# GpSimd subtracts each weight chunk's low half in four operations of 256 columns instead of one of 1024

## What is computed

```
x += 0.5 * SwiGLU_a(rms(x))
P = rms(x) @ w_in                      # one projection for all branches
A = retention(P[ret]);  B = SSD / Mamba-2(P[ssm]);  C = RWKV-7(P[rwkv])
x += w_out( sum_i sigmoid(P[gate_i]) * (branch_i @ w_branch_i) )
x += CrossAttn(rms(x), memory K/V)
x += 0.5 * SwiGLU_b(rms(x))
```

## Time and profile before

| what | value |
|---|---|
| profiled execution, its own time | 3634.34 us |
| span of that execution | 3632.8 us |
| mean granted TensorE clock | 0.922 |
| TensorE matmul busy | 3066.9 us (84%) |
| VectorE busy | 1950.2 us (54%) |
| ScalarE busy | 1166.7 us (32%) |
| GpSimd busy | 536.3 us (15%), of it 430.1 us in L675 |

### The profile page before, as it was taken

How to read it: one execution, slowest core, us unless ns; L and a number is a source line. 1 busy time by engine, 2 the same in 40 slices (tenths; PEclk the granted TensorE clock), 3 DMA queues, 4 the chain that set the end, 5 groups by cost and what they waited for, 6 DMA issues and landing times. The chain is left out here.

```text
span 3632.8 us, 63834 instructions
## 1 busy us (share of the span) xinstructions
PE 3066.9 (84%) x25648; PEld 2795.0 (77%) x25648; DVE 1950.2 (54%) x2906; ACT 1166.7 (32%) x1579; POOL 536.3 (15%) x337
## 2 busy tenths in 40 slices
PE   8999788877787889699989997888777869887997
PEld 7989577676576888499989895776765759885997
DVE  4437565584556455344344376665845655553543
ACT  4432421042121444244244324211421313432542
POOL 0005330143220000000000063201422200000000
PEclk9999899997798999899989998999988979999998
DMA  4434310124162445334344443101332724453442
GB/s 163 148 131 143 95 57 3 48 93 147 61 253 107 145 173 186 128 128 149 117 142 146 135 140 100 40 3 58 107 130 61 271 82 168 170 189 128 133 150 102
DMA packets 119680, 448.00 MB, mean 123 GB/s; under 512 B 13648, under 2 KB 23920, under 8 KB 112176
## 3 DMA queue, kind: packets, MB, share of 16 engines
q1 hardware_dynamic: 98496, 331.84, 27.9%
q0 software_dynamic: 20976, 113.24, 8.0%
HBM read 397.01 MB, written 48.02 MB: 123 GB/s over the span
## 5 line engine op out<-in xcount | busy, mean ns | idle before, releaser
L1359 ACT ACTIVATE w_high<-ring 128x1024 fp32r<-128x1024 f32 x598 | 632.0, 1057 | 953.2 <-PE gemm_banks L823 619.6
L821 PE MATMUL gemm_banks<-in_high,w_high 128*128 128x320 f32 (+1 forms) x2784 | 871.9, 313 | 78.0 <-POOL w_low L675 30.3
L822 PE MATMUL gemm_banks<-in_low,w_high 128*128 128x320 f32 (+1 forms) x2784 | 860.6, 309 | 0.0
L823 PE MATMUL gemm_banks<-in_high,w_low 128*128 128x320 f32 (+1 forms) x2784 | 860.2, 309 | 0.0
L1700 DVE TENSOR_TENSOR w_low<-ring,w_high 128x1024 fp32r<-128x1024 f32 x436 | 534.0, 1225 | 543.1 <-ACT w_high L1359 539.2
L821 PEld LDWEIGHTS gemm_banks<-in_high,w_high 128*128 128x128 f32 x2784 | 529.8, 190 | 95.0 <-issue 72.6
L675 POOL TENSOR_TENSOR w_low<-ring,w_high 128x1024 fp32r<-128x1024 f32 x162 | 430.1, 2657 | 1102.3 <-ACT w_high L1359 587.7
L822 PEld LDWEIGHTS gemm_banks<-in_low,w_high 128*128 128x128 f32 x2784 | 530.3, 190 | 1.1
L823 PEld LDWEIGHTS gemm_banks<-in_high,w_low 128*128 128x128 f32 x2784 | 529.5, 190 | 0.0
L861 PE MATMUL gemm_banks<-in_high,w_high 128*128 128x320 f32 x640 | 227.3, 355 | 76.1 <-ACT stage L1427 37.4
L813 PE MATMUL gemm_banks<-in_high,w_high 128*128 128x320 f32 (+1 forms) x656 | 210.7, 334 | 69.2 <-ACT in_high L1375 66.0
(11 more groups left out here) (383 smaller groups left out, 4530.8 us busy)
## 6 DMA issues: line engine op xcount, KB each, us to landing
ring<-in_w SPq DMA_DIRECT2D x602, 512.0 KB, 3.3
arena<-in_kc POOLq DMA_DIRECT2D x16, 1024.0 KB, 7.0
arena<-in_vc POOLq DMA_DIRECT2D x16, 1024.0 KB, 9.1
out_fill<-stage SPq DMA_DIRECT2D x80, 160.0 KB, 3.8
arena<-out_fill POOLq DMA_DIRECT2D x4, 2560.0 KB, 11.1
arena<-in_ssm POOLq DMA_DIRECT2D x16, 512.0 KB, 10.4
out_s_ssm<-arena POOLq DMA_DIRECT2D x16, 512.0 KB, 7.0
arena<-in_ret POOLq DMA_DIRECT2D x16, 512.0 KB, 23.2
```

The costliest lines, as they stand in the source:

```text
L821: mm(dst, w_high[:, slot, w(k)], in_high[:, k, 0:n], start=(k == 0), stop=False)
L822: mm(dst, w_high[:, slot, w(k)], in_low[:, k, 0:n], start=False, stop=False)
L823: ins_ = mm(dst, w_low[:, slot, w(k)], in_high[:, k, 0:n], start=False, stop=(k == KT - 1))
L1359: f(w_high[:, slot], ring[:, s, 0:D], ACT.Copy).then_inc(weights_high, 1)
```

## The change

The one subtraction of 1024 columns becomes four of 256, written one behind the other. Only the first has the wait for ScalarE's copy in front of it, and only the last raises `weights_split`, so TensorE is released at the same point of the work as before: when the whole chunk is subtracted. What VectorE subtracts is left as it is.

```diff
+PIECES = 4
@@ weights (GpSimd)
                 slot = RANK[pos] % AHEAD
                 pool.wait_ge(weights_high, i * unit + (RANK[pos] + 1))
-                nc.gpsimd.tensor_tensor(w_low[:, slot], ring[:, pos % RING, 0:D], w_high[:, slot].bitcast(F32),
-                                        ALU.subtract).then_inc(weights_split, 1)
+                for q in range(PIECES):
+                    c = slice(q * D // PIECES, (q + 1) * D // PIECES)
+                    ins_ = nc.gpsimd.tensor_tensor(w_low[:, slot, c], ring[:, pos % RING, c], w_high[:, slot, c].bitcast(F32),
+                                                   ALU.subtract)
+                ins_.then_inc(weights_split, 1)
```

## The result

The kernel with four pieces took 3646.86 us (median of 10 runs, 3639.19 to 3662.03) against 3639.51 for the kernel before on the same chip (10 runs). The ratio is 1.0026, 95% interval 1.0014 to 1.0039: 9.5 us slower, 5 to 14. The forecast was 33 us slower; the side was right, the size was not.

The account below looks back on a forecast made before the run. It took chunk matmuls, ScalarE's copy and GpSimd's subtraction as the bounding loop, with GpSimd and VectorE taking turns. Terms 10.8 + 7.0 + 9.0 + 7.0 = 33.8 us on 3634.3 gave 3668 us, range 3640 to 3702.

Parts of the forecast that it names:

- f = 0.15 us: Fixed cost of each added GpSimd operation; three more per chunk cost 0.45 us.
- The rival that the next piece starts up for nothing: GpSimd starts each piece while the last runs, no fixed cost, only turns: 3643 us, chance 0.15.
- Projection +10.8: In the `rwkv` projection, 24 chunk starts waiting for the subtraction each come 0.45 us later: 10.8 us.
- `prepare_rwkv`, +7.0: RWKV preparation: start -1.9, middle +1.0, end +4.4, making 3.5 us per layer, 7.0 for both.
- L1833 ends 1.8 us earlier and the sum L933 starts 1.9 us earlier: Preparation's start: VectorE waits 4.4 us instead of 6.1, so TensorE's waiting sum gains 1.9 us per layer.
- The middle, +1.0: Preparation's middle: four turns with L1844 make a fill 1.6 us late, of which the next column sum passes on 1.0.
- The end, +4.4: Preparation's end: pieces wait for L1862 and L1863, the fill starts 5.1 us late; 4.4 per layer after VectorE's lead.
- Headnorm's end and `ssm`, +9.0: Headnorm's end and the `ssm` projection: a start 2.1 us late plus later waits, 4.5 us per layer, 9.0 for both.
- 7 x 0.45 = 3.2: In the `ssm` projection, seven starts of L821 waiting for the subtraction each come 0.45 us later, per layer.
- Scan, +7.0: SSD scan: six L2033 groups 1.8, `z` load 0.9, two end fills 0.8; 3.5 us per layer, 7.0 for both.
- each of the four waits for one piece: the same 2.2 us in all: SSD scan: four L2033 operations wait as long together as one did for a whole subtraction, plus 0.3 us fixed per group.
- the one with VectorE's gain: Shorter VectorE waits at L933 and headnorm's end gain 5.4 us per layer: kernel faster at 3623 us, chance 0.10.

Follow-up runs that it names:

- proj: Four pieces only in the 26 chunks of the rwkv projection, whole elsewhere, against the kernel before: 1.0030, +11 us (6 to 16).
- e_end: Four pieces only in chunks 13 and 14 of the rwkv fills, beside VectorE's two great reductions, against the kernel before: 1.0029, +11 us (6 to 15).
- ssm: As a run: four pieces only in the 13 chunks of the ssm projection, against the kernel before: 1.0023, +8 us (4 to 12).
- sfill: Four pieces only in the 20 fill chunks in the SSD scan and first 2 of ret, against the kernel before: 0.9996, -1.5 us (-7 to +4).
- rfill: Four pieces only in the 20 fill chunks beside RWKV preparation and headnorm, against the kernel before: 1.0011, +4 us (-1 to 9).
- e_front: Four pieces only in chunks 2 to 4 of the rwkv fills, against the kernel before: 0.9979, -8 us (-13 to -3).
- e_mid: Four pieces only in chunks 5 to 12 of the rwkv fills, against the kernel before: 1.0003, +1 us (-3 to +5).
- before again: The kernel before, executed once more with a profile and no edit: 3636.78 us.
- e_fs: Four pieces only in chunks 2 to 4 of the rwkv fills and beside the SSD scan, against the kernel before: 0.9967, -12 us (-17 to -8).

## Why the forecast was wrong in size, by its own steps

**f = 0.15 us: right.** The shortest operations are 192, 712, 1252 and 2333 ns for 8, 256, 512 and 1024 columns: 2.11 ns a column and 0.17 us fixed. Of the latter some 0.04 overlap with the operation before when it is queued behind one. Four end to end take 2.82 us for 2.41 (forecast 2.75 to 2.85), so three pieces more cost 0.41 us, forecast 0.45. The estimate by the Trainium skill (GPSIMD Engine Reference, Performance versus the Vector engine), 169 ns from its 4497 ns for 2048 columns, agrees with the 0.17. The rival that the next piece starts up for nothing is out but for the 0.04.

**Projection +10.8: right.** +10.0 in the trace to L924, +11 in `proj`. The count behind it was off: 11 starts of a chunk a layer waited for GpSimd before and not 12 (of the 28 of L821 in the earlier trace rows, 12 are here and 16 in `ssm`), and 22 x 0.45 is 9.9. The period went from 7.47 to 7.87 (forecast 8.0), which the pieces' 0.41 us make up alone; nothing of it is left for L1806. What was forecast of it, a maximum under 1 us, was wrong; source view:

```profile
L1806 DVE SCALAR_TENSOR_TENSOR arena<-arena,par x52: 235/554/5761, 280.7 to 2187.9; - x48, 128x8 f32<-128x8 f32 x4
```

its median fell from 1277 to 554 ns, but the longest is 5761.

**`prepare_rwkv`, +7.0: +1.6 in the trace** (-5.4 + 6.2 and -5.5 + 6.3). The step that failed is "L1833 ends 1.8 us earlier and the sum L933 starts 1.9 us earlier". L1833 (now L1837) ended 3.3 us earlier against L1829's start, and the sum, its gap of 3.55 us gone, ran at a granted clock of 1.00, the upper level of 2.4 GHz. The windows are of before over 420.20 to 427.50 and of after over 419.70 to 424.27, each from the sum's start to the same matmul of the fill behind it; the columns are us, busy time of PE, PEld, DVE, ACT and POOL, granted clock, DMA share, GB/s:

```profile
420.20:427.50 7.30, 7.30 (x12) 3.25 (x13) 0.00 (x0) 0.00 (x0) 2.15 (x1) 0.64 0.03 7
```

```profile
419.70:424.27 4.57, 4.57 (x14) 2.18 (x13) 0.00 (x0) 1.38 (x2) 4.57 (x7) 1.00 0.54 154
```

that is 2.7 us more, which the forecast left out. The middle, +1.0, came out at -0.6: from the start of L1839 to that of L1860 (now L1864) it took 35.2 us for 35.8. The eight L1848 take 7.50 us for 10.85 (eight turns at 0.35 for three at 2.1), but a fill there waits 3.09 us for the chunk itself, at 450.50, where the earlier trace rows have 2.11. The end, +4.4, was a real loss, and larger. The walk itself was right to 0.1 us: against the start of L1860 (now L1864) the fill came at 10.69 us for 5.09, 5.6 later. But that fill, behind 7.23 us of idle time, ran at the lower clock, so the next one was 6.8 later and not 5.1. RWKV's start came 6.8 later too; with the middle's -0.6 these are the stage's 6.2. In `e_end`, with pieces in the end's two chunks alone, layer 1 has 6.9.

**Headnorm's end and `ssm`, +9.0: +4.3 in the trace, +8 (4 to 12) in `ssm` alone.** The start at 758.55 was further off than the 2.1 forecast. The last fill ahead of the projection already starts 3.5 us later than before (753.36 for 749.87) and that start 8.1 later (766.66), so 4.6 belong to this place, 2.5 of them to the first chunk's lower clock, 6.19 us for 3.68. Then the step "7 x 0.45 = 3.2" failed: the waits behind that start did not grow, their sum fell from 11.5 to 9.8 us. The convolution's first 45 operations on VectorE take 34.2 us for 38.4; that TensorE's waits fell by way of ScalarE's copies, which follow them, fits this but no run shows it apart. The 0.8 that I took back for this was too little. `ssm` timed alone, though, leaves the 9.0 inside its interval.

**Scan, +7.0: -10.7 in the trace, -1.5 (-7 to +4) timed alone.** This is the step with the largest error, and it has the wrong sign in the trace: "each of the four waits for one piece: the same 2.2 us in all". A group of four meets three turns, and a turn costs VectorE 0.35 us, not 0.55. So about half of a piece's 0.71 us goes by beside VectorE's operation. That is more than its fixed 0.17, and which part of it that is, no run shows. Before, one turn was 1.6 us where L2033 takes 352 ns alone (four of them took 1.96 us), now three are 1.0. For TensorE that is 2.1 us over both layers: its matmuls of L1104 waited 47.0 us for L2033 before and wait 44.9 for L2037 now. From the source views of the two, before and after:

```profile
  PE gemm_banks L1104: 26.3, 6
...
  PE mixer_banks L1104: 20.7, 10
```

```profile
  PE gemm_banks L1108: 23.0, 6
  PE mixer_banks L1108: 21.9, 11
```

So the scores, forecast at +3.6 for both layers, came to -2.1. These 2.1 are the edit's: `sfill` has the same 44.9, and `proj`, `ssm`, `rfill`, `e_front` and `e_mid`, with whole chunks there, have 46.9 to 47.2. Most of the 10.7 is something else, and the forecast had no term for it: TensorE is busy 8.0 us less over the same work (windows over the scan of both layers, before and after):

```profile
sum 362.30, PE 283.26 PEld 232.32 DVE 190.12 ACT 75.97 POOL 86.66; mean PE 141.63 PEld 116.16 DVE 95.06 ACT 37.98 POOL 43.33
```

```profile
sum 351.62, PE 275.28 PEld 226.55 DVE 183.61 ACT 75.97 POOL 111.92; mean PE 137.64 PEld 113.28 DVE 91.81 ACT 37.98 POOL 55.96
```

It goes with a granted clock of 0.82 and 0.83 in place of 0.79 and 0.80. An unedited kernel can have a part of this by chance: in layer 1 "before again" is busy for 140.0 us for 143.2, at 0.80. The five kernels with four pieces there are alike, -6.9 to -7.6 in layer 1 and -3.3 to -4.5 in layer 2; the seven with whole chunks have -3.2 to 0.0 and -0.3 to +3.1, so with the clock the edit's share is some 4 to 6 us a layer in the traces. Timed, it is -1.5 us (-7 to +4) by itself and -4 from `e_front` to `e_fs`, which is nearer to the 2.1 of the waits alone. Whether the shorter waits bring the better clock with them, and why the times show so little of it, stays open.

**Of the rivals**, the one with VectorE's gain had a place and the mechanism of what came: L933, worth 5.4 us a layer rather than 1.9. It was wrong on the point from which it decides: the fills behind L1862 were late, and it was outweighed. GpSimd didn't keep VectorE out through all four pieces: L1866 and L1867 got in between.

The sum by the trace: 10.0 + 1.6 + 4.3 - 10.7 = 5.2, -1.9 in the lora and +5.2 in the other stages, of which the forecast had neither: 8.5 in all. At the two places where shorter holds count most, the front and the scan, the forecast had -3.8 + 7.0 = +3.2 and the trace -10.9 - 10.7 = -21.6. That is 25 us, as much as the error of the whole sum; the other terms' errors cancel each other but for 0.5. By the runs' times the scan's part of it is smaller.

## What to carry to other kernels

Where two engines take turns, as GpSimd and VectorE do here, cutting one's operation makes each of its pieces wait for one of the other engine's operations. So ask at each place who is late: cut where the other engine's chain is waited for and its operations are short (0.35 us a turn for it here), and keep whole where the matmuls wait for the cut operation beside operations of 2.8 us. The same edit was worth -8 us in three chunks a layer and +11 us in two others; chosen by place it made the kernel 16 to 20 us faster, everywhere alike 9.5 slower. A gap in TensorE can cost twice, as L933's did here: 3.55 us idle and 2.7 more at the lower clock. So a wait removed or added there is to be priced with the matmuls behind it.

## What the runs showed of the hardware

- GpSimd's subtraction of two fp32 tensors takes 0.17 us and 2.11 ns per column of 128 partitions (8 to 1024 columns). Of the 0.17, 0.14 remain for each operation that is queued behind another.
- A turn costs VectorE less than the piece it lets by: 0.35 us for one of 0.71, about 1.6 to 2.1 for a whole one of 2.33. To GpSimd a turn costs nearly VectorE's whole operation: a piece takes 3306 ns for 712 beside an operation of 2.83 us.
- Behind a gap of 3.55 us L933's sum and the fill's first matmuls ran with a granted clock of 0.64 on the mean and took 7.30 us; without the gap they ran at 1.00 and took 4.57 us.
- Two executions of the same kernel differed by 5.6 us in one stage and by 2.4 in all. Whether a subtraction starts 0.2 us before an operation of VectorE or 0.1 us behind it decides a turn of 2.1 us.
